# Moving the first chunk's convolution taps on TensorE behind the third chunk's first slab

## The reference, cut to what matters

```python
def conformer_conv(x, hist, norm_g, w_pw1, b_pw1, conv_w, conv_b, ln_g, ln_b, w_pw2):
    a, g = jnp.split(rmsnorm(x, norm_g) @ w_pw1 + b_pw1, 2, axis=-1)
    u = a * jax.nn.sigmoid(g)
    y, new_hist = causal_dwconv(u, hist, conv_w)          # 31 taps, one filter per channel
    y = layernorm(y + conv_b, ln_g, ln_b)
    return jax.nn.silu(y) @ w_pw2, new_hist
```

## Time and profile before

| | |
|---|---|
| median of 3 runs | 1469.98 us (1463.07 to 1470.7) |
| profiled execution, its span | 1461.8 us |
| its mean granted TensorE clock | 0.989 |
| TensorE matmuls busy | 1395.3 us (95%) |
| weight loads on TensorE busy | 1299.8 us (89%) |
| VectorE busy | 720.4 us (49%) |
| ScalarE busy | 479.2 us (33%) |
| GpSimd busy | 596.9 us (41%) |

### The profile page before, as it was taken

How to read it: one execution, slowest core, us unless ns; L and a number is a source line. 1 busy time by engine, 2 the same in 40 slices (tenths; PEclk the granted TensorE clock), 3 DMA queues, 4 the chain that set the end, 5 groups by cost and what they waited for, 6 DMA issues and landing times.

```text
span 1461.8 us, 34670 instructions
## 1 busy us (share of the span) xinstructions
PE 1395.3 (95%) x14005; PEld 1299.8 (89%) x14005; DVE 720.4 (49%) x1256; ACT 479.2 (33%) x706; POOL 596.9 (41%) x329
## 2 busy tenths in 40 slices
PE   6998998988999999999999999988999999999998
PEld 5896767767999999999999977757999999999998
DVE  5646888874535443024442376667365430144411
ACT  4375333322333222222223321227433321222221
POOL 3322333322426554445543364422255554355441
PEclk9999999999999999999999999999999999999999
DMA  6417899979323222333312566542223323332122
GB/s 185 130 54 243 296 327 322 366 270 307 94 64 96 86 79 87 94 89 90 90 57 69 143 164 157 148 115 60 69 87 90 90 76 90 101 87 86 54 84 74
DMA packets 246246, 192.56 MB, mean 132 GB/s; under 512 B 12129, under 2 KB 205106, under 8 KB 246058
## 3 DMA queue, kind: packets, MB, share of 16 engines
q1 hardware_dynamic: 244561, 188.31, 41.9%
q10 hardware_dynamic: 1181, 1.44, 0.4%
q0 software_dynamic: 400, 1.32, 0.3%
HBM read 173.03 MB, written 6.04 MB: 122 GB/s over the span
## 4 chain that ended last, share of the span: by engine, by line
PE 74%; DVE 3%; issue 2%; ACT 1%; DMA 0%; POOL 0%; SPq 0%; ACTq 0%; DVEq 0%; POOLq 0%
PE banks L1810 64%; PE banks L2243 2%; PE banks L2076 2%; PE banks L1827 1%; PE banks L2015 1%; PE banks L1957 1%; PE banks L2192 1%; DMA u_sh<-u 0%; DVE k_grp L1300 0%; SPq L610 0%; ACTq L1106 0%; PE banks L2048 0%; PE banks L1965 0%; PE banks L2246 0%; DVE sb L1363 0%
## 5 line engine op out<-in xcount | busy, mean ns | idle before, releaser
L683 POOL TENSOR_TENSOR w_l<-w_raw,w_h 128x1024 fp32r<-128x1024 f32 (+2 forms) x195 | 439.3, 2255 | 411.9 <-ACT w_h L830 397.1
L1810 PE MATMUL banks<-xa_h,w_h 128*128 128x272 f32 x1856 | 388.1, 290 | 4.4 <-DVE tmp L1633 3.3
L1810 PE MATMUL banks<-xa_h,w_l 128*128 128x272 f32 x1856 | 385.2, 289 | 0.0
L1810 PE MATMUL banks<-xa_l,w_h 128*128 128x272 f32 x1856 | 383.6, 288 | 0.0
L1810 PEld LDWEIGHTS banks<-xa_h,w_h 128*128 128x128 f32 x1856 | 292.9, 189 | 6.7 <-issue 5.5
L1810 PEld LDWEIGHTS banks<-xa_l,w_h 128*128 128x128 f32 x1856 | 292.3, 189 | 0.0
L1810 PEld LDWEIGHTS banks<-xa_h,w_l 128*128 128x128 f32 x1856 | 290.4, 189 | 0.0
L830 ACT ACTIVATE w_h<-w_raw 128x1024 fp32r<-128x1024 f32 (+2 forms) x193 | 185.1, 961 | 200.2 <-PE banks L1810 199.9
L1810 PE MATMUL banks<-h_h,w_h 128*128 128x272 f32 x928 | 193.1, 289 | 0.3 <-DVE x L1572 0.3
L1810 PE MATMUL banks<-h_h,w_l 128*128 128x272 f32 x928 | 192.6, 289 | 0.0
L1810 PE MATMUL banks<-h_l,w_h 128*128 128x272 f32 x928 | 191.9, 288 | 0.0
(11 more groups left out here) (302 smaller groups left out, 1650.8 us busy)
## 6 DMA issues: line engine op xcount, KB each, us to landing
w_raw<-in_w_up SPq DMA_DIRECT2D x88, 512.0 KB, 3.7
k_grp<-in_cache_k SPq DMA_DIRECT2D x128, 256.0 KB, 4.4
v_pg<-in_cache_v SPq DMA_DIRECT2D x120, 256.0 KB, 5.1
w_raw<-in_w_in SPq DMA_DIRECT2D x24, 512.0 KB, 6.4
w_raw<-in_w_down SPq DMA_DIRECT2D x32, 384.0 KB, 3.1
w_raw<-in_w_pw SPq DMA_DIRECT2D x24, 512.0 KB, 3.7
w_raw<-in_w_down SPq DMA_DIRECT2D x32, 320.0 KB, 3.0
w_raw<-in_w_out SPq DMA_DIRECT2D x8, 512.0 KB, 5.6
```

Of the source, the lines that this page charges most:

```text
L683: g.tensor_tensor(w_l[:, slot, 0:n], w_raw[:, slot, 0:n], w_h[:, slot, 0:n].bitcast(F32), ALU.subtract).then_inc(s_lo, 1)
L1810: ins = mm(out[:, half, 0:HT], w, v[:, half * HT:(half + 1) * HT], start=first and t == 0 and n == 0, stop=last and t == phase.tiles - 1 a ...
```

## The change

The taps of chunk 0 no longer follow slab 3 but slab 4. Turn 1 is now written out too, and the loop starts at turn 2. Nothing else is changed: the order of the other engines, the buffers and the waits stay as they are.

```diff
-            def gemm(phase, moving, ready, between=None, after_two=None, then=None, late=None):
+            def gemm(phase, moving, ready, between=None, after_two=None, then=None, late=None, second=None):
...
                     if j == 0 and between:
                         between()
-                    if after_two and j % 2:
-                        after_two(0, j // 2)
                 if then:
                     then()
-                with pe.Fori(1, phase.turns - (1 if late else 0)) as i:
+                if second:
+                    for j in range(4):
+                        slab(phase, 1, j, moving)
+                        second(j)
+                with pe.Fori(2 if second else 1, phase.turns - (1 if late else 0)) as i:
                     for j in range(4):
                         slab(phase, i, j, moving)
                         if after_two and j % 2:
...
             def conv_before(i, b):
 
-                if isinstance(i, int) and b == 0:
-                    return
                 pe_conv(i * 2 + (b - 1), 1 - b, i + (b - 1))
-            gemm(ph["pw1"], xa, xa_ready(NORM["down01"]), sums("down01"), conv_before)
+
+            def first_convs(j):
+
+                if j != 2:
+                    c = (j + 1) // 2
+                    pe_conv(c, c % 2, c // 2)
+            gemm(ph["pw1"], xa, xa_ready(NORM["down01"]), sums("down01"), conv_before, second=first_convs)
```

## The result

The kernel with the change takes 1471.75 us, the median of 17 runs (1466.21 to 1478.38). The kernel before, in 17 runs beside them, takes 1468.12 us (1463.07 to 1473.07). The ratio is 1.0027, with an interval of 1.0015 to 1.004: the change makes the kernel about 4 us slower, where a gain of 1.3 us was forecast; the time lies 0.75 us above the upper end of the forecast's range. The profiled execution of after has a span of 1470.3 us against 1461.8. Of these 8.5 us, 5.68 are there already when S3 ends (854.72 before, 860.40 after), which is ahead of everything that the change moves.

A forecast was written before the change was run, and what follows sets the result against it. TensorE was taken as the bound. Terms -3.11 - 1.67 + 0.83 + 1.5 + 1.6 - 0.36 leave -1.2 us (1.3 by starts), so 1469.98 - 1.3 = 1468.7 us, range 1460.2 to 1471.0.

The forecast's parts named there:

- Bound: Whole kernel: TensorE bounds it, its matmuls being busy for nearly the whole span.
- gain to be had: TensorE at chunk 0's taps: a 3.11 us wait plus 1.67 us of slow clock, 4.78 us in reach.
- S4: Slab 4 on TensorE, moved ahead of chunk 0's taps: a new wait of 0.83 us for VectorE to read its PSUM pair.
- T0: Taps of chunk 0 on TensorE: no wait for copies, 4.98 us at full clock, ending 2.13 us later than before.
- T1: Taps of chunk 1 on TensorE: a wait of 1.5 us for copies, leaving TensorE 2.5 us ahead.
- VectorE, chunk 1: VectorE's sum and taps of chunk 1: GpSimd's low 8 and tap weights 2 get in the way, costing 2.0 us.
- rival A: Tap weights 2 on GpSimd wait for VectorE's taps to end, keeping a gain of 2.9 us: 1467.1 us; chance 0.32.
- T2: Taps of chunk 2 on TensorE: a wait of 1.6 us for copies, starting 0.95 us ahead of before.
- After T2: Chunks after chunk 2's taps: VectorE, with 3.32 us of idling, catches up by chunk 3; later waits move with TensorE.
- the jump: The loop's jump back ahead of slab 8, gone with turn 1 written out: 0.36 us gained.
- B: Clock falls at a new gap on TensorE; at chunk 2's taps nothing absorbs 1.67 us: 1470.4 us; chance 0.13.
- C: Nothing moves: the old wait ahead of chunk 0's taps is accidental or replaced by one as long; 1469 to 1470; chance 0.10.

The follow-up runs named there:

- e4: The changed kernel, with GpSimd waiting before the second and fourth low part of a turn until VectorE has read the value slab behind its taps; ratio 0.9994.
- e7: The changed kernel, with GpSimd waiting ahead of the even tap weights and ahead of the fourth low part of a turn; 1464.08 us, ratio 0.9983.
- e3: The kernel before, with three adds of 512 columns on VectorE once, ahead of the taps of chunk 1; ratio 1.0003.
- e9: The kernel before, with eight adds of 512 columns on VectorE once, ahead of the taps of chunk 1; 1474.07 us, ratio 1.005.
- e5: The kernel before, with three small extra GpSimd operations behind the first low part of a pair in two turns; 1475.97 us, ratio 1.0067.
- e2: The changed kernel, with GpSimd's tap weights 2, 4 and 6 waiting until VectorE has read the value slab behind its taps; 1464.85 us, ratio 0.9986.

## Why the prediction was wrong

**Bound, gain to be had, S4 and T0: right.** S4 0.93 for 0.83, T0 4.98 us at full clock.

**T1: right, a little high.** The wait is 1.03 us for 1.5; it starts 12.2 us after T0 and not 12.6.

**VectorE, chunk 1: right.** High 8 follows high 7, tap weights 2 meet VectorE right behind low 8 and cost it 1.6 us (2.0 forecast). It was the sum that stood and not the first tap, the case named as "or just miss it". Less the 5.68 us by which S3 ends later, the taps end at 877.0 (876.9 forecast). Against rival A, tap weights 2 took 1.91 us and did not wait. The Trainium skill (SBUF — State Buffer, section "SBUF: two separate sides") has a pair of ports shared by VectorE and GpSimd, locked by whichever starts first for a whole instruction; this trace agrees, with 0.13 us between the two starts (873.71 and 873.84). It gives no rule for what follows here, who is served when one engine works without a break and the other arrives.

**T2: mechanism right, size high.** u of chunk 2 is there at 885.97, the 880.3 of the forecast plus the 5.68 us by which S3 ends later. From there T2 starts 11.85 us on, where 10.86 + 1.8 were put down: SyncE's 16 issues took 10.05 us here. T2 waits 0.88 for 1.6. At this point the new order is 1.7 us ahead, more than the 0.95 forecast.

**After T2: this step failed.** The prediction says that "VectorE waits for TensorE in each chunk (3.32 us of idling at 876.83), so it catches up by chunk 3, and every later wait moves with TensorE". The 3.32 us are a row of the old order, where VectorE has read the value slab early and S5 is late. In the new order VectorE comes to that pair of reads 4.2 us later (882.62 for 872.79, less 5.68) and S5 is done 3.7 us earlier (878.71 for 876.72). So at 883.25 it reads the gate slab without any wait, and the slack is gone. I relied on a slack that the change itself uses up, although the numbers for it stood in the T2 step: S5 done at 872.7 and read at 877.55. And I looked at GpSimd only up to tap weights 2. What is left of the two shifts, low 9 0.7 us later and low 10 2.7 us earlier, more than halves GpSimd's idling ahead of low 10, and from there chunks 2 to 4 cost VectorE 5.2 to 5.4 us more each (3.8 for two taps, 1.4 to 1.6 for the sum). TensorE waited 1.17 and 2.02 us ahead of T3 and T4, where the forecast has none. e4 takes the meetings out of the taps of the new order, e7 all but one, and the lead stays; e3 and e9 show in the old order that a delay within the slack vanishes and one beyond it doesn't, e9 with a larger delay than meant and with TensorE ahead.

**The sum, as measured.** -3.11 - 1.67 as forecast; +0.93, +1.03, +0.88 for the first three waits (3.93 forecast, 2.84 measured); -0.36 for the jump. That alone is -2.3, where the forecast had -1.2. Then come the terms that the forecast put at nothing: +1.17 + 2.02 for T3 and T4 and +1.68 for T4's slow clock. All together that is +2.6. The profiled executions say +2.86 at T7; the rest, 0.3, isn't broken down. The two clock terms cancel here; in another execution they needn't.

**Rivals.** B has the right sign and the right mechanism (the clock falls at a new gap and nothing absorbs it), but at T4, a gap that it didn't know. A's gain of 2.9 us is what the order yields when GpSimd doesn't stop the taps, but in after it did. C fell: the wait ahead of T0 is 3.0 to 3.1 us in all six profiled executions of the old order.

**Chances.** Slower had 0.04, because no case gave more than 1.5 us of loss. None of them asked whether a meeting can cause the next one. The measured loss, 0.27%, is inside the half per cent called the same; the comparison of 17 runs each resolved it all the same.

## What to carry to other kernels

When a change moves one engine ahead and another back, subtract both shifts from the slack row before relying on it, and follow the third engine for two more rounds: its work hangs partly on the one and partly on the other, and so its instructions move against each other. Where VectorE and GpSimd meet, a delay can feed itself for some rounds (three here, five in e9): VectorE late, GpSimd's idling shorter, two more instructions stopped, VectorE later. A wait that places GpSimd's work behind VectorE's long streak made this order 2.9 us faster in the phase; without it the order lost.

## What the runs showed of the hardware

What decides whether a GpSimd instruction that arrives in VectorE's unbroken streak stops it? I went through the arrivals of low parts in VectorE's taps (and adds) in ten traces, leaving out those that follow another GpSimd instruction at once. After idling of 1.82 to 4.44 us all 18 stopped VectorE for about 2.1 us, 17 at the next instruction and one an instruction later (e5, idling of 3.17); a nineteenth, after only 0.83 us (e5, 951.45), did too. (The expectation of e5 says 9 and 22 for the traces until then; counted this way they are 8 and 21.) After idling of 4.77 to 6.36 us none of 28 did: they took 3.17 to 5.46 us and got in only when the streak was over. The place in the streak doesn't separate them (an arrival in the seventh tap stopped it after 4.11 us in e2, and not after 6.11 in e3). GpSimd instructions right behind one that had got in stopped another tap every time. e5 was made to test this and agrees, but it changed more than the idling, so it is a regularity and no shown cause. It is not general either. The running sum, which mostly starts 0.21 us behind the instruction before it, was stopped at 888.30 of the kernel after by a low part that had idled for 11.99 us. And in pw2 of the kernel before, a low part that had idled for 14.92 us (1060.27) stopped an instruction of 32 columns, 2.40 us at 1060.76, in a sequence with other operands and small gaps. Why, stays open.

The clock fell after 2.02 us of idling ahead of T4 and stayed up after 1.17 ahead of T3; but it stayed up after T5's 2.02 us in e5 too. T0 of the old order shows it best: its wait is 3.0 to 3.1 us in all six profiled executions, and it ran slow behind it in five of them, but at full clock in e9 (columns as in the earlier trace rows):

```profile
857.78 1.07 PE L2250 MATMUL banks<-u_sh,w_sh 128*32 128x512 f32 x8 [3.04 <-DMA u_sh<-u]
857.90:861.90 4.00, 4.00 (x72) 1.60 (x72) 3.96 (x3) 0.68 (x3) 4.00 (x3) 1.00 0.48 135
```

In the same 4 us the granted clock was 0.62 in before, where the wait was 3.11. So here as in the earlier trace rows the length of the gap alone doesn't decide, and the 1.67 us that the forecast counted as gained at T0 are there in some executions only.
